# Attention scores as three products of rounded parts, transpositions one step later, and the first gates rounded earlier

## The chip, the cores and the metric

One core of a Trainium2 chip runs the whole kernel in one launch. TensorE multiplies, VectorE and ScalarE work element by element and empty TensorE's accumulation banks (PSUM, four pairs of 1024 columns), GpSimd (POOL) adds a little, and SyncE (SP) issues most transfers. Each engine works off its own list in order and waits for the others by semaphores. The metric is the device time of the kernel in microseconds, the median of several runs. Matrix operands are 32-bit floats in two kinds of product: plain fp32, and fp32r, a faster form with a shorter significand.

## The reference, cut to what matters

The kernel computes two layers of a hybrid trunk for 512 latent tokens and 128 context tokens of width 1024. In each layer a modulated norm feeds one wide projection; four mixers run on its parts (attention A, a gated recurrence B, differential attention C, a gated recurrence D); their outputs are projected, gated and merged, and a convolutional feed-forward part follows. The change is in the two attentions:

```python
s = jnp.einsum('bqgrd,bkgd->bgrqk', qblk.astype(jnp.float32), kf) * scale
p = jax.nn.softmax(s, axis=-1)
return jnp.einsum('bgrqk,bkgv->bqgrv', p, vf)
```

A latent query sees 512 latent keys and 256 cached ones (768), a context query the 128 context keys. A has four heads of 64 channels; C has four heads, each with two softmaxes of 32 channels whose difference weighs the values.

## The kernel before

**Products of parts.** The large matrix products take each fp32 operand as a rounded value (hi) plus its rest (lo), both fp32r, and add hi x hi, hi x lo and lo x hi. ScalarE writes a weight's hi, VectorE the rest. Products with few columns, the attention scores among them, are plain fp32. Only a weight that has been loaded, rounded and subtracted can be used: `early_unit(n)` (ScalarE) and `early_lo(n)` (VectorE) do that for the first six gate weights, one unit of 1024 columns each.

**The attention loop.** The attentions of one layer are 30 steps g = 6 i + u: five blocks i of 128 queries, and six jobs u, the first two for pairs of heads of A, the other four for heads of C. Each step has two score matrices, one per accumulation pair 0 and 1, and their operands lie on different partitions (64 rows each for A, 32 for C). Steps 0 to 23 have 768 keys, steps 24 to 29 have 128. A step's work goes:

- `scores(g)` on TensorE, when the exponentials of step g - 1 have read both score pairs (L1004: 512 latent keys, L1006: 256 cached keys, L1001: context);
- `maxima(g)` on VectorE, the negated maximum of each row (L2143);
- `exponentials(g)` on ScalarE, with the row sums (L1569);
- `normalise(g)` on VectorE (L2150 to L2156); a step of C combines its two matrices to one, a step of A keeps two;
- `turn(g, first)` and, for u = 0 and 1, `turn(g, second)` on TensorE: transposition by blocks of 128 into pair 2 (L1019), each of which waits until ScalarE has copied the one before (`keep_turned`, L1581);
- `weigh(g)` on TensorE, except for u = 2 and 4, whose turn is weighed with the next one: the values are weighed into the lower half of pair 3 (L1035); `outputs` copies them out (VectorE, L2161).

**What fills TensorE between them.** The first six of the gate products, 16 parts each (eight per half of the 640 tokens, a part being three fp32r products of 320 columns, L971 to L973), are done in between. All halves go to the upper half of pair 3 (`HALF_GATE`), so each waits for ScalarE's copy of the half before (L1560, `gates_kept`). `FIRST_FILL` parts go ahead of the loop, and `GATE_FILL` says how many at two places in each step. What is left follows the loop. Behind the stage comes the merge (L791 to L793).

**Order on the engines**, written out by hand. TensorE in step g:

```python
scores(g); turn(g - 2, 1); weigh(g - 3); gate_fill(g, 0); turn(g - 1, 0); gate_fill(g, 1)
```

ScalarE: copies of finished halves (with the next unit's rounding), `keep_turned(g - 2, 1)`, `exponentials(g)`, `keep_turned(g - 1, 0)`. VectorE: the rest of a unit if due, `outputs` if due, `normalise(g - 1)`, `maxima(g)`. Ahead of the loop, in and behind the last projection chunk, run `decay(d)` and `decay_in(d)`, which make the decay factors of mixer D through a chain of ScalarE and VectorE operations that ends at L1546; the loops of ScalarE and VectorE begin behind it. `ada_turn` and `modulation_late` finish a conditioning row; the first gate part waits for the latter (L1977).

Of the kernel before, what the change touches and what calls it, by code (L numbers as in the profile page):

```python
# [8 lines left out]
ALU = mybir.AluOpType  # L9
# [3 lines left out]
P = 128  # L13
D = 1024
KT = D // P
# [188 lines left out]
GATE_FILL, FIRST_FILL = ((0, 2), (1, 2), (1, 2)), 8  # L204
# [45 lines left out]
def halves_before(g):  # L250

    return min(2 * N_EARLY, (FIRST_FILL + sum(sum(GATE_FILL[i % 3]) for i in range(g))) // KT)
# [35 lines left out]
def build(nc, A, O):  # L288
    ctx = ExitStack()
    with ctx:  # L290
# [9 lines left out]
        def sem(name):  # L300
# [123 lines left out]
        W_FIRST = W_EARLY, BIG_R[:, 4608:4864]  # L424
        MIX_AT = NG - 2
# [26 lines left out]
        s_full, nmax_ready, p_ready, normed_p, pt_full, pt_kept, pv_done, o_taken = (  # L452
            sem(n) for n in ("s_full", "nmax_ready", "p_ready", "normed_p", "pt_full", "pt_kept", "pv_done", "o_taken"))
# [25 lines left out]
        HALF_GATE = PS[:, 3, 512:512 + HALF]  # L479

# [281 lines left out]
        def _(pe):  # L762
# [3 lines left out]
            for l in range(DEPTH):  # L766
# [190 lines left out]
                decay(1)  # L957
                if turned is not None:
                    ada_turn(turned)

                def gate_parts():

                    for n in range(N_EARLY):
                        w_hi, w_lo = tiles_of(W_GATE[(EARLY + n) % N_SLOT]), raw(RING_R, EARLY + n, 0, P, P, KT)
                        for h, (a, b, _) in enumerate(HALVES):
                            if h == 0:
                                lo_ready(U_MIX + n)
                            if n + h:
                                pe.wait_ge(half_kept, l * 2 * N_EARLY + 2 * n + h)
                            for k in range(KT):  # L970
                                release(pe.matmul(HALF_GATE, w_hi[:, k, :], h_hi(k)[:, a:b], start=k == 0, stop=False), h + k == 0)  # L971
                                pe.matmul(HALF_GATE, w_hi[:, k, :], h_lo(k)[:, a:b], start=False, stop=False)
                                ins = pe.matmul(HALF_GATE, w_lo[:, k, :], h_hi(k)[:, a:b], start=False, stop=k == KT - 1)  # L973
# [6 lines left out]
                def gate_fill(g, n):  # L980
                    for _ in range(GATE_FILL[g % 3][n]):
                        next(gates, None)
# [9 lines left out]
                def scores(g):  # L992
# [334 lines left out]
        def _(act):  # L1327
# [17 lines left out]
            for l in range(DEPTH):  # L1345
# [134 lines left out]

                def head_inv_root(i):
# [5 lines left out]
                for c in range(NC_Z):  # L1487
                    for n, (g, kind, dst, j) in enumerate(Z_TILES[c]):
# [38 lines left out]
                def early_unit(n):  # L1527
                    chunk_in(EARLY + n)
                    act.activation(W_GATE[(EARLY + n) % N_SLOT], RING[:, (EARLY + n) % N_SLOT, 0:1024], ACT.Copy).then_inc(hi_made, 1)

                early_unit(0)
# [10 lines left out]
                act.dma_start(O["keysT"][at].rearrange("l p a t -> p (l a) t"), ZT[:, AK:AK + 3, TS:T]).then_inc(stored, 16)  # L1542
                act.dma_start(O["vals"][at].rearrange("l p n -> p (l n)"), V_AC[:, NT - 1, :]).then_inc(stored, 16)
# [6 lines left out]
                def gates_kept(count):  # L1550

                    nonlocal halves
                    while halves < count:
                        n, h = divmod(halves, 2)
                        act.wait_ge(half_gate, l * 2 * N_EARLY + halves + 1)
                        if h == 0 and n + 1 < N_EARLY:
                            early_unit(n + 1)
                        if n == 4 and h == 0:
                            act.wait_ge(gate_sent[0], l * 16 + 16)
                        act.activation(LOGIT[n][:, HALVES[h][0]:HALVES[h][1]], HALF_GATE, ACT.Copy).then_inc(half_kept, 1)  # L1560
# [33 lines left out]
                act.wait_ge(al_ready, l * 2 + 2)  # L1594
                for g in range(NG + 3):
# [3 lines left out]
                    keep_turned(g - 2, 1)  # L1599
# [1055 lines left out]
```

## Time and profile before

| what | value |
|---|---|
| median of 3 runs | 2473.71 us (2473.59 to 2474.51) |
| the profiled execution's own time | 2473.59 us |
| its span | 2471.8 us |
| TensorE products busy | 2369.9 us, 96% of the span |
| VectorE, ScalarE, GpSimd busy | 60%, 41%, 12% |
| mean granted clock of TensorE | 0.989 |

The span is the time from the first to the last instruction. In the timeline a row is a start, a duration, an engine, a source line and what was written from what; rows of TensorE overlap, since the duration holds the way through the array, so the difference of two starts tells what a product costs. An fp32 product leaves two records. A bracket is idle time of that engine ahead of the row, and whose work ended it.

### The profile page before, as it was taken

Reading aid. Unit: us, or ns where it says so; the run is one execution under the profiler, and the core shown is the slowest. Engines: PE = TensorE matmul, PEld = TensorE weight load, DVE = VectorE, ACT = ScalarE, POOL = GpSimd, SP = SyncE. Lnnn points to the kernel's source line nnn. Section 1 sums busy time; section 2 is a strip of 40 time slices with the busy share of each in tenths; the row PEclk is TensorE's granted clock in tenths of the full one; section 3 lists DMA queues with packets and bytes.
Section 4 is the critical chain, followed back from the end, with each engine's and each line's share of the span. In section 5 each row is a group of like instructions: output and inputs, shape, how many; then the busy total and the mean of one; then the engine's idle time right before and its main releaser. Section 6 shows DMA issues by size and latency. Waiting matters only on the chain. (4 is left out here: it accounts for less than half of the span.)

```text
span 2471.8 us, 49604 instructions
## 1 busy us (share of the span) xinstructions
PE 2369.9 (96%) x21594; PEld 2209.5 (89%) x21594; DVE 1489.5 (60%) x2274; ACT 1014.9 (41%) x1408; POOL 305.6 (12%) x203
## 2 busy tenths in 40 slices
PE   5999899999999999999989998999999999999998
PEld 4999777889999899999989996788899989999998
DVE  4134476986744788883241436777775658888621
ACT  4245465322252555551143536642212545555410
POOL 0000000000000545530000000000000006555000
PEclk8999999999999999999999999999999999999999
DMA  8555111222246223333244331121222633332321
GB/s 276 186 169 172 51 33 46 59 54 54 60 144 186 79 81 87 86 105 91 75 145 128 119 104 38 33 69 44 55 66 83 207 104 86 86 86 75 103 81 66
DMA packets 326509, 239.32 MB, mean 97 GB/s; under 512 B 18272, under 2 KB 317344, under 8 KB 325024
## 3 DMA queue, kind: packets, MB, share of 16 engines
q1 hardware_dynamic: 317584, 211.32, 29.3%
q10 hardware_dynamic: 8720, 24.99, 2.9%
q8 instruction: 162, 2.65, 0.4%
q14 instruction: 43, 0.35, 0.0%
HBM read 220.68 MB, written 15.60 MB: 96 GB/s over the span
## 5 line engine op out<-in xcount | busy, mean ns | idle before, releaser
L791 PE MATMUL PS<-HH_split,WHI_split 128*128 128x320 f32 x1952 | 616.5, 316 | 12.0 <-DVE HL_split L2017 10.4
L793 PE MATMUL PS<-HH_split,RING_split 128*128 128x320 f32 x1920 | 594.6, 310 | 0.0
L792 PE MATMUL PS<-HL_split,WHI_split 128*128 128x320 f32 x1760 | 545.9, 310 | 0.0
L791 PEld LDWEIGHTS PS<-HH_split,WHI_split 128*128 128x128 f32 x1952 | 368.3, 189 | 24.3 <-issue 13.2
L2042 DVE TENSOR_TENSOR RING_split<-RING,WHI_split 128x1024 fp32r<-128x1024 f32 (+2 forms) x154 | 222.7, 1448 | 270.1 <-ACT WHI_split L1710 183.2
L793 PEld LDWEIGHTS PS<-HH_split,RING_split 128*128 128x128 f32 x1920 | 361.8, 188 | 0.0
L792 PEld LDWEIGHTS PS<-HL_split,WHI_split 128*128 128x128 f32 x1760 | 332.6, 189 | 0.3
L792 PE MATMUL PS<-ZT_split,WHI_split 128*128 128x320 f32 x1032 | 320.5, 311 | 0.0
L741 POOL TENSOR_TENSOR BIG<-HH_split,HL_split 128x640 f32<-128x640 f32 x8 | 14.3, 1824 | 1760.1 <-DVE HL_split L2014 1760.1
L2049 DVE TENSOR_TENSOR RING_split<-RING,WHI_split 128x1024 fp32r<-128x1024 f32 x52 | 62.2, 1223 | 226.3 <-ACT WHI_split L1408 225.9
L792 PEld LDWEIGHTS PS<-ZT_split,WHI_split 128*128 128x128 f32 x1032 | 195.4, 189 | 0.0
L1242 PE MATMUL PS<-BIG_split,WHI_split 128*128 128x320 f32 x576 | 178.0, 309 | 0.0
L791 PE MATMUL PS<-V_split,WHI_split 128*128 128x320 f32 x480 | 151.8, 316 | 1.8 <-DVE RING_split L2042 1.8
L793 PE MATMUL PS<-V_split,RING_split 128*128 128x320 f32 x488 | 152.0, 312 | 0.0
L1710 ACT ACTIVATE WHI_split<-RING 128x1408 fp32r<-128x1408 f32 x32 | 44.1, 1379 | 220.9 <-PE PS L793 168.6
L1241 PE MATMUL PS<-V_split,WHI_split 128*128 128x320 f32 x432 | 133.7, 309 | 0.0
L1646 ACT ACTIVATE WHI<-PS 128x640 f32<-128x640 f32 x48 | 33.8, 705 | 223.9 <-PE PS L793 223.5
L1569 ACT ACTIVATE BIG<-PS,NMX 128x768 f32<-128x768 f32 (+1 forms) x120 | 94.1, 791 | 74.0 <-DVE NMX L2143 73.9
L1242 PEld LDWEIGHTS PS<-BIG_split,WHI_split 128*128 128x128 f32 x576 | 108.1, 188 | 0.0
L2246 DVE COPY_PREDICATED BIG<-MASK,PS 128x640 f32<-128x640 uint8 x96 | 84.5, 881 | 34.9 <-PE PS L1121 34.7
L2143 DVE TENSOR_REDUCE NMX<-PS 128x1 f32<-128x768 f32 (+1 forms) x120 | 93.2, 818 | 15.9 <-PE PS L1006 12.8
L1609 ACT ACTIVATE WHI_split<-RING 128x1280 fp32r<-128x1280 f32 (+1 forms) x54 | 67.0, 1241 | 68.1 <-PE PS L793 68.1
(321 smaller groups left out, 5493.8 us busy)
## 6 DMA issues: line engine op xcount, KB each, us to landing
RING<-in_w_in SPq DMA_DIRECT2D x96, 512.0 KB, 4.0
RING<-in_w_up SPq DMA_DIRECT2D x88, 512.0 KB, 5.0
RING<-in_w_ada SPq DMA_DIRECT2D x80, 512.0 KB, 6.1
RING<-in_w_down SPq DMA_DIRECT2D x32, 384.0 KB, 3.6
RING<-in_w_in SPq DMA_DIRECT2D x40, 256.0 KB, 3.3
RING<-in_w_down SPq DMA_DIRECT2D x32, 320.0 KB, 4.0
RING<-in_w_out SPq DMA_DIRECT2D x16, 512.0 KB, 4.8
ZT<-in_w_ada SPq DMA_DIRECT2D x8, 1024.0 KB, 9.3
```

The lines of the kernel that those rows point to most:

```text
L791: release(pe.matmul(out, w_hi, hi[:, a:b], start=begin, stop=False), fresh and a == 0)
L792: pe.matmul(out, w_hi, lo[:, a:b], start=False, stop=False)
L793: ins = pe.matmul(out, w_lo, hi[:, a:b], start=False, stop=end)
L1241: release(pe.matmul(out, w_hi[k], hi[:, k, :], start=not onto and k == 0, stop=False, skip_group_check=onto), fresh and k == 0)
L1242: pe.matmul(out, w_hi[k], lo[:, k, :], start=False, stop=False, skip_group_check=onto)
L1569: act.activation(PROB[g % 3][m][:, 0:n], pair(m)[:, 0:n], ACT.Exp, bias=NMX[:, g % 3, m:m + 1], accum_out=SUMS[:, g % 3, m:m + 1]).then_in ...
L1609: act.activation(W2[m % 2][:, 0:width], RING[:, (MIX + m) % N_SLOT, 0:width], ACT.Copy).then_inc(hi_made, 1)
L1710: act.activation(W_DN[q % 2], RING[:, (DOWN + q) % N_SLOT, 0:11 * P], ACT.Copy).then_inc(hi_made, 1)
L2042: nv.tensor_tensor(rest, value, as_f32(hi), ALU.subtract).then_inc(lo_made, 1)
L2049: nv.tensor_tensor(z_raw(RING_R, l, c, j), z_raw(RING, l, c, j), as_f32(w_z(u, 256 if kind in ("t4", "t1") else P)), ALU.subtract).then_in ...
L2143: nv.tensor_reduce(NMX[:, g % 3, m:m + 1], pair(m)[:, 0:keys(g // NS) * P], AX.X, ALU.max, negate=True).then_inc(nmax_ready, 1)
L2246: ins = nv.copy_predicated(SCORE[:, h], m, ps)
```

## The change

The scores of the steps with 768 keys become three products of parts: keys and queries are rounded to hi, their rests written in place. The keys (three tiles, a latent and a cached piece each) and the first three queries are rounded in the last projection chunk, the others in the loop; the space of the keys' hi comes from weight buffers and from a state array, whose one block is cleared again in `states`. The first two gate weights are rounded in that chunk too. The second half of the first gate goes to the upper half of pair 2, and its eight parts go behind the first scores. In each step the transpositions come one step later, and the weighing behind them; VectorE takes the maxima ahead of the normalisation. Two stores that ScalarE issues move into the loop.

```diff
-GATE_FILL, FIRST_FILL = ((0, 2), (1, 2), (1, 2)), 8
+FIRST_FILL = 8
+GATE_FILL = ((8, 0),) + ((0, 2), (1, 2), (1, 2)) * 8 + ((0, 2),) * 8
...
+        K_TILE = (AK, CK, CK + 1)
+        K_HI = [(WHI_R[:, 3072:3584], WHI_R[:, 3584:3840]), (BIG_R[:, 4608:5120], WHI_R[:, 3840:4096]),
+                tuple(ST_R[:].rearrange("p (d x n) -> p d x n", d=2, x=3)[:, 0, x, 64:320] for x in (slice(0, 2), 2))]
+        K_LO = [(ZT_R[:, t, 0:TS], CACHE_R[:, PAST * n:PAST * n + PAST]) for n, t in enumerate(K_TILE)]
+        Q_HI = [ST_R[:, 960 + 320 * b:960 + 320 * b + P] for b in range(3)]
...
+        SECOND_HALF = PS[:, 2, 512:512 + HALF]
+        def half_out(n, h):
+            return SECOND_HALF if (n, h) == (0, 1) else HALF_GATE
...
 @@ TensorE, behind the projection
-                decay(1)
                 if turned is not None:
                     ada_turn(turned)
+                decay(1)
 @@ TensorE, gate_parts
-                            if n + h:
+                            if n:
                                 pe.wait_ge(half_kept, l * 2 * N_EARLY + 2 * n + h)
 @@ TensorE, scores
-                    for m in range(2):
-                        pe.matmul(pair(m)[:, 0:TS], ZT[r[m], q, ti], ZT[r[m], k, 0:TS], start=True, stop=True)
-                    for m in range(2):
-                        pe.matmul(pair(m)[:, TS:TS + PAST], ZT[r[m], q, ti], KTC[r[m], kc, :], start=True, stop=True).then_inc(s_full, 1)
+                    n = q_at(i, u)
+                    if g == 0:
+                        pe.wait_ge(k_lo, l * 6 + 6)
+                    pe.wait_ge(q_lo, l * N_Q + (n + 1))
+                    q_hi_part, q_lo_part = Q_HI[n % 3], ZT_R[:, q, ti]
+                    for part, out in ((0, slice(0, TS)), (1, slice(TS, TS + PAST))):
+                        hi_part, lo_part = K_HI[kc][part], K_LO[kc][part]
+                        for first, (qp, kp) in zip((True, False, None), ((q_hi_part, hi_part), (q_hi_part, lo_part), (q_lo_part, hi_part))):
+                            for m in range(2):
+                                ins = pe.matmul(pair(m)[:, out], qp[r[m]], kp[r[m]], start=first is True, stop=first is None)
+                                if first is None and part == 1:
+                                    ins.then_inc(s_full, 1)
 @@ TensorE, turn
                     if t:
                         pe.wait_ge(pt_kept, l * NTURN + t)
+                    else:
+                        pe.wait_ge(half_kept, l * 2 * N_EARLY + 2)
 @@ TensorE, loop over the steps
-                    turn(g - 2, 1)
+                    turn(g - 3, 1)
+                    gate_fill(g, 0)
+                    turn(g - 2, 0)
                     weigh(g - 3)
-                    gate_fill(g, 0)
-                    turn(g - 1, 0)
                     gate_fill(g, 1)
 @@ ScalarE, last projection chunk, behind its first tile
                             decay_in(0)
+                            early_unit(0)
+                            keys_hi()
+                            for k in range(3):
+                                query_hi(k)
+                            early_unit(1)
 @@ ScalarE, loop over the steps
-                    keep_turned(g - 2, 1)
+                    keep_turned(g - 3, 1)
                     if g < NG:
                         exponentials(g)
-                    keep_turned(g - 1, 0)
+                    keep_turned(g - 2, 0)
+                    if q_made(g) is not None:
+                        query_hi(q_made(g))
+                    if g == 3:
+                        act.dma_start(O["keysT"][at].rearrange("l p a t -> p (l a) t"), ZT[:, AK:AK + 3, TS:T]).then_inc(stored, 16)
+                    if g == 4:
+                        act.dma_start(O["vals"][at].rearrange("l p n -> p (l n)"), V_AC[:, NT - 1, :]).then_inc(stored, 16)
+                    if early < N_EARLY and 2 * early - 1 <= halves_before(g):
+                        early_unit(early)
+                        early += 1
  @@ VectorE, loop over the steps
-                    while early < N_EARLY and 2 * early - 1 <= halves_before(g - 1):
+                    if g > NS and g % NS == 3:
+                        outputs(g // NS - 1, 1)
+                    if g < NG:
+                        maxima(g)
+                    if g:
+                        normalise(g - 1)
+                    if g % NS == 5:
+                        outputs(g // NS, 0)
+                    if g and q_made(g - 1) is not None:
+                        query_lo(q_made(g - 1))
+                    if early < N_EARLY and 2 * early - 1 <= halves_before(g - 1):
                         early_lo(early)
                         early += 1
-                    if g % NS == 5:
-                        outputs(g // NS, 0)
-                    if g > NS and g % NS == 3:
-                        outputs(g // NS - 1, 1)
-                    if g:
-                        normalise(g - 1)
-                    if g < NG:
-                        maxima(g)
 @@ VectorE, states
+                    if x + d == 0:
+                        step.mark(nv.memset(ST[:, 0, :, NT - 1, :], 0.0))
```

In `gate_parts` the products write `half_out(n, h)` in place of `HALF_GATE`. `early_unit(0)` stood behind the last projection chunk, `early_unit(n + 1)` in `gates_kept`, the two stores ahead of ScalarE's loop. VectorE runs `early_lo(0)`, `keys_lo()`, three `query_lo` and `early_lo(1)` where ScalarE runs their counterparts; `early_lo(0)` stood behind the chunk too. The new `keys_hi` and `query_hi` are copies on ScalarE (six pieces, 512 and 256 columns; a query 128), `keys_lo` and `query_lo` the subtractions on VectorE. `q_made(g)` names the query that step g rounds, at u = 0, 1, 3 and 5.

## Rows read from the trace of the kernel before

**Rows 1.** The page's first line: span and instructions.

```profile
span 2471.8 us, 49604 instructions
```

**Rows 2.** Timeline, TensorE, steps 19 and 20: start, us, engine, line, operation, count, idle time.

```profile
380.83 1.13 PE L1004 MATMUL PS<-ZT 64*128 64x512 f32 x4
...
385.35 1.13 PE L1004 MATMUL PS<-ZT 32*128 32x512 f32 x4 [0.78 <-ACT BIG L1569]
386.31 0.60 PE L1006 MATMUL PS<-CACHE,ZT 32*128 32x256 f32 x4
386.84 0.87 PE L1019 MATMUL PS<-CONST,BIG 128*128 128x128 f32 x6
387.64 1.09 PE L1035 MATMUL PS<-WHI,V 128*64 128x128 f32 x16
...
389.10 0.41 PE L971 MATMUL PS<-HH_split,RING_split 128*128 128x320 f32 x1
...
389.65 0.82 PE L1019 MATMUL PS<-CONST,BIG 128*128 128x128 f32 x6
390.22 0.39 PE L971 MATMUL PS<-HH_split,RING_split 128*128 128x320 f32 x1
...
391.28 0.70 PE L1004 MATMUL PS<-ZT 32*128 32x512 f32 x2
```

**Rows 3.** Timeline, TensorE: first scores of steps 0, 1, 2, 6, 24; the merge's first product.

```profile
282.42 1.13 PE L1004 MATMUL PS<-ZT 64*128 64x512 f32 x4
...
289.53 2.08 PE L1004 MATMUL PS<-ZT 64*128 64x512 f32 x4 [2.64 <-ACT BIG L1569]
...
295.51 1.13 PE L1004 MATMUL PS<-ZT 32*128 32x512 f32 x4
...
315.61 0.70 PE L1004 MATMUL PS<-ZT 64*128 64x512 f32 x2 [0.78 <-ACT BIG L1569]
...
406.34 0.49 PE L1001 MATMUL PS<-ZT 64*128 64x128 f32 x4 [0.79 <-ACT BIG L1569]
...
428.83 0.42 PE L791 MATMUL PS<-HH_split,WHI_split 128*128 128x320 f32 x1 [0.53 <-ACT WORK L1560]
```

**Rows 4.** Stretch table: us, busy time of each engine, granted clock, DMA share, GB/s.

```profile
280.00:290.00 10.00, 5.58 (x33) 4.25 (x34) 4.97 (x7) 7.25 (x12) 0.00 (x0) 0.88 0.32 93
```

**Rows 5.** Timeline, VectorE, step 19: the two maxima.

```profile
382.43 1.82 DVE L2143 TENSOR_REDUCE NMX<-PS 128x1 f32<-128x768 f32 x2 [0.26 <-PE PS L1006]
```

**Rows 6.** Timeline, TensorE, input projection: products three apart, of 320 and 256 columns.

```profile
149.72 0.31 PE L791 MATMUL PS<-HH_split,WHI_split 128*128 128x320 f32 x1
...
150.16 0.31 PE L791 MATMUL PS<-HH_split,WHI_split 128*128 128x320 f32 x1
...
154.88 0.28 PE L914 MATMUL PS<-RING_split,HH_split 128*128 128x256 f32 x1
...
155.24 0.28 PE L914 MATMUL PS<-RING_split,HH_split 128*128 128x256 f32 x1
```

**Rows 7.** Timeline, TensorE: one fp32 product of 512 columns alone.

```profile
275.21 1.12 PE L780 MATMUL PS<-ZT,WAL 32*128 32x512 f32 x2
```

**Rows 8.** Timeline, weight loads of TensorE, scores of step 19.

```profile
380.83 0.30 PEld L1004 LDWEIGHTS PS<-ZT 64*128 64x128 f32 x4 [0.30 <-ACT BIG L1569]
381.37 0.19 PEld L1006 LDWEIGHTS PS<-CACHE,ZT 64*128 64x128 f32 x2 [0.24 <-issue]
```

**Rows 9.** Timeline, TensorE, step 2: two transpositions without a weighing between them.

```profile
297.00 0.88 PE L1019 MATMUL PS<-CONST,BIG 128*128 128x128 f32 x6
297.63 0.39 PE L971 MATMUL PS<-HH_split,RING_split 128*128 128x320 f32 x1
...
298.87 0.84 PE L1019 MATMUL PS<-CONST,BIG 128*128 128x128 f32 x6 [0.55 <-ACT WHI L1581]
```

**Rows 10.** Timeline, ScalarE and VectorE: the last projection tile.

```profile
275.32 0.70 ACT L1500 ACTIVATE ZT<-PS 128x640 f32<-128x640 f32 x1 [4.97 <-PE PS L793]
...
276.05 0.82 DVE L2112 TENSOR_TENSOR ZT<-ZT,PS 128x640 f32<-128x640 f32 x1 [6.22 <-ACT ZT L1500]
```

More of the change, by code:

```diff
@@ L202 @@
 NG = NT * NS
-GATE_FILL, FIRST_FILL = ((0, 2), (1, 2), (1, 2)), 8
+FIRST_FILL = 8
+GATE_FILL = ((8, 0),) + ((0, 2), (1, 2), (1, 2)) * 8 + ((0, 2),) * 8
+assert FIRST_FILL + sum(map(sum, GATE_FILL)) == 16 * N_EARLY
 TURN0 = [8 * (g // NS) + (0, 2, 4, 5, 6, 7)[g % NS] for g in range(NG)] + [8 * NT]
@@ L250, in halves_before @@
 def halves_before(g):
-    return min(2 * N_EARLY, (FIRST_FILL + sum(sum(GATE_FILL[i % 3]) for i in range(g))) // KT)
+    return min(2 * N_EARLY, (FIRST_FILL + sum(sum(GATE_FILL[i]) for i in range(g))) // KT)
 def keys(i):
@@ L424, in build, with q_at, q_made @@
         W_FIRST = W_EARLY, BIG_R[:, 4608:4864]
+        K_TILE = (AK, CK, CK + 1)
+        K_HI = [(WHI_R[:, 3072:3584], WHI_R[:, 3584:3840]), (BIG_R[:, 4608:5120], WHI_R[:, 3840:4096]),
+                tuple(ST_R[:].rearrange("p (d x n) -> p d x n", d=2, x=3)[:, 0, x, 64:320] for x in (slice(0, 2), 2))]
+        K_LO = [(ZT_R[:, t, 0:TS], CACHE_R[:, PAST * n:PAST * n + PAST]) for n, t in enumerate(K_TILE)]
+        K_RAW = [(ZT[:, t, 0:TS], KTC[:, n, :]) for n, t in enumerate(K_TILE)]
+        Q_TILES = (AQ, AQ + 1, CQ, CQ + 1)
+        Q_HI = [ST_R[:, 960 + 320 * b:960 + 320 * b + P] for b in range(3)]
+        N_Q = 4 * (NT - 1)
+        def q_at(i, u):
+            return 4 * i + (0, 1, 2, 2, 3, 3)[u]
+        def q_made(g):
+            i, u = divmod(g, NS)
+            k = {0: 4 * i + 3, 1: 4 * i + 4, 3: 4 * i + 5, 5: 4 * i + 6}.get(u)
+            return k if k is not None and k < N_Q else None
         MIX_AT = NG - 2
@@ L980, in gate_fill @@
                 def gate_fill(g, n):
-                    for _ in range(GATE_FILL[g % 3][n]):
+                    for _ in range(GATE_FILL[g][n]):
                         next(gates, None)
@@ L1479, in decay_in, with early_unit, keys_hi, query_hi @@
                     act.activation(SQ[d], pair(2)[:, 0:T], ACT.Abs, bias=COLS[:, C_AB + d:C_AB + d + 1]).then_inc(al_lin, 1)
+                def early_unit(n):
+                    chunk_in(EARLY + n)
+                    act.activation(W_GATE[(EARLY + n) % N_SLOT], RING[:, (EARLY + n) % N_SLOT, 0:1024], ACT.Copy).then_inc(hi_made, 1)
+                def keys_hi():
+                    act.wait_ge(params_in, (l + 1) * N_PARAM)
+                    for n in range(3):
+                        for part in range(2):
+                            out, raw_part = K_HI[n][part], K_RAW[n][part]
+                            if n == 2 and part == 0:
+                                raw_part = raw_part.rearrange("p (x n) -> p x n", n=PAST)
+                            act.activation(out, raw_part, ACT.Copy).then_inc(k_hi, 1)
+                def query_hi(k):
+                    i, t = divmod(k, 4)
+                    act.activation(Q_HI[k % 3], ZT[:, Q_TILES[t], i * P:(i + 1) * P], ACT.Copy).then_inc(q_hi, 1)
                 def head_inv_root(i):
@@ L2101, in head_rotary, with early_lo, keys_lo, query_lo @@
                     nv.tensor_tensor(ZT[:, t, 0:TS], TMP[0][:, 0:TS], TMP[1][:, 0:TS], ALU.add).then_inc(qk_done, 1)
+                def early_lo(n):
+                    lo(U_MIX + n, RING_R[:, (EARLY + n) % N_SLOT, 0:1024], RING[:, (EARLY + n) % N_SLOT, 0:1024], W_GATE[(EARLY + n) % N_SLOT])
+                def keys_lo():
+                    for n in range(3):
+                        for part in range(2):
+                            rest, value, hi_part = K_LO[n][part], K_RAW[n][part], K_HI[n][part]
+                            if n == 2 and part == 0:
+                                rest, value = (x.rearrange("p (x n) -> p x n", n=PAST) for x in (rest, value))
+                            v.wait_ge(k_hi, l * 6 + (2 * n + part + 1))
+                            nv.tensor_tensor(rest, value, as_f32(hi_part), ALU.subtract).then_inc(k_lo, 1)
+                def query_lo(k):
+                    i, t = divmod(k, 4)
+                    at = slice(i * P, (i + 1) * P)
+                    v.wait_ge(q_hi, l * N_Q + (k + 1))
+                    nv.tensor_tensor(ZT_R[:, Q_TILES[t], at], ZT[:, Q_TILES[t], at], as_f32(Q_HI[k % 3]), ALU.subtract).then_inc(q_lo, 1)
                 sig = 0
@@ L2119, in _ @@
                             head_round_rest(c - QK_AT - 2)
+                        if c == NC_Z - 1 and n == 0:
+                            early_lo(0)
+                            keys_lo()
+                            for k in range(3):
+                                query_lo(k)
+                            early_lo(1)
                     if l + c == 0:
```

27 lines of the change are left out of this document (9 added, 18 removed).

## The prediction, written before the result was known

> **What bounds the kernel now.** I read the page first, then the chain of waits, then the timeline of the attention stage, the only stage that the change alters. The span is 2471.8 us [rows 1], and the profiled execution took 2473.59 us, 1.79 us more; the median of the runs is 2473.71, so the sum below, made against 2473.59, is good for the median to 0.1 us. TensorE is busy nearly everywhere, so time saved in one stage goes straight to the end, if TensorE doesn't wait there instead. In the first layer the stage runs from 282.42 us to the first product of the merge at 428.83; the second layer repeats it, step by step, and I count it twice.
>
> Two limits alternate from step to step. In step 19 TensorE has little to do and waits 0.78 us for the exponentials [rows 2]: scores, two maxima of 1.82 us [rows 5], two exponentials, and only then the next scores, because both score buffers are in use. That loop is 385.35 - 380.83 = 4.52 us, of which 1.49 are the scores (385.35 to 386.84 in step 20), so everything else in it is 3.03. In step 20 TensorE is full: scores 1.49, transposition 0.80, weighing 1.46, one gate part 0.55, transposition 0.57, two parts 1.06, together 5.93, and no wait [rows 2]. Steps 6 to 23 take 406.34 - 315.61 = 90.73 us, 30.24 for six [rows 3]. The start of the stage is worse: steps 0 to 5 take 33.19, because step 0 takes 7.11 and step 1 5.98 [rows 3]. Before step 1 TensorE waits 2.64 us; the granted clock in this stretch is 0.88 [rows 4], and the first scores of step 1 take 2.08 us where those of step 2 take 1.13, nearly the ratio of the 1.2 and 2.4 GHz levels. The reader is to see a stage with four wait-free steps in six [rows 2, 3], and a start with a stall and a slow stretch after it.
>
> **The scores by parts.** One step's scores are now four fp32 products in two pairs, the two of a pair on different rows of the array. A pair of 512 columns takes 385.35 to 386.31, 0.96 us, and the pair of 256 to 386.84, 0.53 [rows 2]. A single fp32 product of 512 columns takes as long as such a pair: 1.12 us in its row [rows 7] against 1.13. So the two of a pair run side by side. Of the 0.96, 0.11 is the first weight load (four loads of 0.19 begin within 0.11 [rows 8]) and 0.85 the stream, 2048 column cycles at 2.4 GHz; of the 0.53, 0.43 is stream and 0.10 the change to the next shape.
>
> The change makes six pairs of these two, in fp32r. Three fp32r products take 0.44 us at 320 columns and 0.36 at 256 [rows 6], 0.147 and 0.120 each, so about 0.42 ns a column more: 0.228 at 512. No fp32r product on part of the rows is in this trace. From below: 0.11 + 3 x 0.213 + 3 x 0.107 + 0.10 = 1.17 us, streams without any gap. From above, if pairs stay side by side with the gaps of the full array: 0.11 + 3 x 0.228 + 3 x 0.120 + 0.10 = 1.25. If 0.11 and 0.10 were both hidden, 1.04. If pairs don't run side by side at all, 0.11 + 6 x 0.213 + 6 x 0.107 + 0.10 = 2.13. I take 1.20, since the rows of the fp32 pairs show neither a gap nor a lost overlap. That is 0.29 less than 1.49.
>
> The loads for the 256-column products begin at 381.37, in the middle of the 512-column streams on the same rows, which end at about 381.8 [rows 2, 8]; so I count only the first load. The Trainium skill has a rule that speaks against this ("TensorE: Matmul & The Clock Gate", Part 3: Packing small matmuls, row/col tiling): a weight load overlaps products in flight only when it goes to another row group. By that rule every pair's loads would be exposed, and the sum would be rival C's; the trace disagrees.
>
> **Transpositions one step later.** What was transposition (second), weighing, parts, transposition (first) becomes transposition (second of g-3), 0 or 1 part, transposition (first of g-2), weighing, two parts. The buffer of the transposed block is single, so the second of two transpositions waits until ScalarE has copied the first. In the old order the weighing of 1.46 us covers the copy. Where it didn't, in step 2, the next transposition starts 1.87 us after the first although only 0.63 + 0.55 lies between them [rows 9]. In the new order nothing but that part covers it in the steps u=3 and u=4 of each six (those with two transpositions). A transposition right ahead of a weighing costs 0.17 more than ahead of a part (0.80 against 0.63 [rows 2, 9]), so 0.74 behind a part or a wait (0.57 + 0.17).
>
> The six steps are then, S being 1.20: u=0 and u=2: S + 0.55 + 0.74 + 1.46 + 1.06 = 5.01 each, TensorE-bound. u=1 and u=5: TensorE has S + 1.69 and S + 2.18, less than the loop, so S + 3.03 = 4.23 each. u=3 and u=4: S + 1.87 + 0.74 + 1.46 + 1.06 = 6.33 each. Together 31.14 against 30.24: 0.90 more for six, though the scores give 6 x 0.29 = 1.74 back; the new wait (0.69 and 1.24 us), and the loop that was reached in two steps already, take it. Three such sixes cost 2.7 us a layer. Maxima ahead of the normalisation take VectorE's normalisation out of the loop; it was beside the scores already, so I count nothing: a gain up to 0.4 us a step if it isn't, and a loss of none.
>
> **The start.** Step 0 gets eight gate parts of 0.44 us (0.147 x 3 [rows 6]) that wait for no copy, since they write another bank. It becomes 1.20 + 3.52 + about 0.1 = 4.8 in place of 7.11; two units of weight are rounded beforehand, so the maxima of step 0 no longer stand behind one. Step 1 becomes the loop, 4.23 in place of 5.98; with TensorE busy through step 0 the clock has no reason in these rows to fall. Step 2 is a loop step too, 4.23; steps 3 to 5 are 6.33 + 6.33 + 4.23. Sum 30.2 against 33.19: 3.0 less a layer.
>
> **Rounding keys and queries.** ScalarE rounds two weight units of 1024 columns (one was rounded here before, just behind the tile), six pieces of keys and three queries; VectorE makes as many subtractions. All lie in the last projection chunk, where ScalarE idles 4.97 us and VectorE 6.22 [rows 10]. At the 640-column rows there, 0.70 and 0.82 us, nine pieces of at most 512 columns are under 6.3 and 7.4 us, by columns (2688) about 3.0 and 3.4; with the units (2048 columns, 2.2 and 2.6) 5.2 and 6.0. They about fit, and the unit no longer rounded behind the tile pays for an overrun. I take 0; from -0.6 to +1.0 a layer. The queries' rounding in the loop (128 columns, 13 a layer on each engine) falls on waits; 0, at worst 13 x 0.2. The two stores that ScalarE issues move from ahead of the stage to steps 3 and 4, behind its work there: 0, at worst 1.3. ada_turn ahead of decay(1): 0. TensorE gets three new waits with its whole order queued behind each: for the rounded keys (done with the chunk), for a query's rest (made two steps or more before its use) and, ahead of the first transposition, for the second half's copy (ScalarE's first work in step 1): none comes last. The fill in states, 192 columns, about 0.25 us a layer on VectorE: 0 to 0.25.
>
> **The end.** Steps 24 on, 406.34 to 428.83 = 22.5 us [rows 3], lose five gate parts (2.2 us) and gain the same kind of waits, short ones. I take -0.7, between -2.2 and +0.5.
>
> **Sum.** -3.0 + 2.7 - 0.7 = -1.0 us a layer, -2.0 for both: 2473.59 - 2.0 = 2471.6 us. All 24 steps carry S once, so each 0.1 us of S is 2.4 us a layer, 4.8 in all. The result is no change that can be told: 0.2%, 4.9 us, is about what a measurement of this kernel tells from none.
>
> **Rivals.**
> *A. Scores at their floor.* With S = 1.05 (load and shape change hidden) the sum is 2471.6 - 7.2 = 2464.4. For it: the loads of a pair begin together [rows 8]. Against: the fp32 pairs don't hide them.
> *B. Weight loads in a row (slower).* In each of the six pairs the loads follow one another, 12 x 0.12 + 0.10 = 1.54: +0.34 x 48 = 16, so 2488. It decides from S = 1.34 upward. For it: fp32r has one load for half the streaming that fp32 had. Against: [rows 8].
> *C. Every load exposed.* If no load went beside a stream on its own rows, the six pairs would each wait 0.11: S = 6 x 0.11 + 0.96 + 0.10 = 1.72, +25, so 2497. Against: [rows 2, 8]. It is what the rule of the skill named above would give.
> *D. Pairs not side by side.* S = 2.13: +45, so 2516. Against: [rows 7].
> *E. The clock falls within the sixes.* TensorE now idles about 1.3, 0.9, 0.7 and 1.2 us in each 31 us. One fall cost 5.98 - 4.52 = 1.5; three a layer make +9, so 2480. Against: no wait there is near 2.64 [rows 3].
> *F. The start isn't gained.* If the rounding ahead delays the decay's exponentials, step 0 stays at 7.11 less 0.29: +2.0 a layer, 2476. This is also the case that the change doesn't do what it says.
>
> **Chances.** The sum 0.40 (its own range 2467 to 2477), A 0.27, B 0.09, C 0.03, D 0.05, E 0.07, F 0.09. Faster by over 0.2%: A and 0.06 of the sum, 0.33. Within: 0.30 of the sum, 0.06 of F and 0.01 of E, 0.37. Slower: 0.04 of the sum, B, C, D, 0.06 of E and 0.03 of F, 0.30. The range runs from 2461, A with a start that gives 1.7 us a layer more, to 2487, just under B; it leaves out C, D and most of B.
>
> **What would show it.** Scores of a step: start to the next operation 1.20 (1.05 A, 1.54 B, 1.72 C, 2.13 D). In steps u=3 and u=4 an idle time of TensorE ahead of the second transposition, put down to ScalarE's copy, 0.7 and 1.2 us. Steps u=1 and u=5 at 4.23. Step 1 starting 4.8 us after step 0 and a granted clock near 1 there. Six steps at 31.1. The prediction is wrong if S is outside 1.13 to 1.34, or if the second transposition doesn't wait.

## The result, and the profile after

The changed kernel takes 2479.76 us (median of 20 executions) against 2474.56 of the kernel before: ratio 1.0026, 95% interval 1.0019 to 1.0032. It is slower by 5.2 us, where no change was forecast; the time lies inside the forecast's range, on rival E's value (2480).

The profiled execution of the changed kernel took 2483.09 us, 3.3 above its median; its span is 9.5 us longer than the one before (to be read beside [rows 1]):

```profile
span 2481.3 us, 50122 instructions
```

The starts of steps 0, 6 and 24 and of the merge in the first layer (timeline of TensorE, beside [rows 3]):

```profile
285.11 0.50 PE L1038 MATMUL PS<-WHI_split,ST_split 64*128 64x512 f32 x2
...
316.40 0.50 PE L1038 MATMUL PS<-WHI_split,ST_split 64*128 64x512 f32 x2 [0.78 <-ACT BIG L1620]
...
412.59 0.38 PE L1027 MATMUL PS<-ZT 64*128 64x128 f32 x2 [0.78 <-ACT BIG L1620]
...
434.71 0.41 PE L817 MATMUL PS<-HH_split,WHI_split 128*128 128x320 f32 x1 [0.53 <-ACT WORK L1611]
```

From the first scores to the merge are 149.6 us, before 146.4; in the second layer 149.3 and 146.4. Ahead of that, the eight gate parts of the first layer ran at half clock in this execution: they start at 278.70, as before, and the scores behind them at 285.11 in place of 282.42. Within the start a second stretch at half clock stands in step 2, behind an idle time of 1.88 us (at full clock a transposition takes 0.8 to 0.9):

```profile
294.33 0.49 PE L1038 MATMUL PS<-BIG_split,ST_split 32*128 32x512 f32 x2 [1.88 <-ACT BIG L1620]
...
297.00 1.48 PE L1055 MATMUL PS<-CONST,BIG 128*128 128x128 f32 x6
```

Steps 19 (its scores and the transposition behind them) and 20, beside [rows 2]:

```profile
384.53 0.50 PE L1038 MATMUL PS<-WHI_split,ST_split 64*128 64x512 f32 x2
...
385.57 0.28 PE L1038 MATMUL PS<-WHI_split,ZT_split 64*128 64x256 f32 x2
385.77 0.33 PE L1055 MATMUL PS<-CONST,BIG 128*128 128x128 f32 x1
...
388.80 0.50 PE L1038 MATMUL PS<-BIG_split,ST_split 32*128 32x512 f32 x2 [1.26 <-ACT BIG L1620]
...
390.61 1.48 PE L1055 MATMUL PS<-CONST,BIG 128*128 128x128 f32 x6
392.02 1.98 PE L1071 MATMUL PS<-WHI,V 128*64 128x128 f32 x16
```

The scores take 385.77 - 384.53 = 1.24 us, close to the 1.20 forecast. But step 20 has a transposition of 1.48 us where others have 0.8 to 0.9, and a weighing of 1.98 where [rows 2] has 1.09. The table by stretches shows why, a granted clock near half (us, then busy time of TensorE, its weight loads, VectorE, ScalarE and GpSimd, then granted clock, DMA share, GB/s; the first stretch is the eight parts, the second this place):

```profile
278.70:285.00 6.30, 6.30 (x24) 6.22 (x24) 1.56 (x2) 4.69 (x7) 0.00 (x0) 0.52 0.33 83
390.00:394.00 4.00, 4.00 (x31) 3.60 (x31) 3.04 (x5) 2.58 (x5) 0.00 (x0) 0.57 0.43 146
```

The new wait stands in steps 21 and 22 (u=3 and u=4) as forecast, the second transposition behind ScalarE's copy of the first:

```profile
396.73 0.87 PE L1055 MATMUL PS<-CONST,BIG 128*128 128x128 f32 x6
...
398.60 0.84 PE L1055 MATMUL PS<-CONST,BIG 128*128 128x128 f32 x6 [0.55 <-ACT WHI L1632]
...
403.16 0.88 PE L1055 MATMUL PS<-CONST,BIG 128*128 128x128 f32 x6
405.02 0.84 PE L1055 MATMUL PS<-CONST,BIG 128*128 128x128 f32 x6 [0.99 <-ACT WHI L1632]
```

In what follows a "six" is the six steps u=0 to u=5, three of them a layer in steps 6 to 23; it is "slow" when one of its steps runs partly at half clock, and "clean" otherwise. Step lengths in us, from the starts of the scores in the timelines:

| kernel | u=0 | 1 | 2 | 3 | 4 | 5 | six |
|---|---|---|---|---|---|---|---|
| before | 4.74 | 4.51 | 5.93 | 5.43 | 5.12 | 4.51 | 30.24 |
| forecast | 5.01 | 4.23 | 5.01 | 6.33 | 6.33 | 4.23 | 31.14 |
| changed | 5.08 | 4.27 | 5.07 | 6.43 | 6.42 | 4.26 | 31.53 |
| changed, slow | 5.08 | 4.27 | 6.67 | 6.43 | 6.42 | 4.26 | 33.13 |

### The profile page after: what moved, and what is told of

It reads as the page before. It is cut to its first block and busy times, and to the rows that moved or that the text cites. A ratio compares the mean times of both kernels' runs of the same rounds, so it can differ in the third digit from the quotient of the medians.

```text
span 2481.3 us, 50122 instructions
## 1 busy us (share of the span) xinstructions
PE 2370.8 (96%) x21786; PEld 2231.7 (90%) x21786; DVE 1496.2 (60%) x2320; ACT 1026.2 (41%) x1452; POOL 305.7 (12%) x203
```

## The experiments

The first group takes the changed kernel and fills or orders TensorE's work otherwise. Ratios are to the kernel before, measured alongside.

**Parts between the transpositions.**

```
-GATE_FILL = ((8, 0),) + ((0, 2), (1, 2), (1, 2)) * 8 + ((0, 2),) * 8
+GATE_FILL = ((8, 0),) + ((0, 2), (1, 2), (3, 0), (2, 0), (1, 2), (1, 2)) * 4 + ((0, 2),) * 8
```

> The changed kernel with one table altered: in the steps u=3 and u=4 all gate parts of the step (three and two) stand between the two transpositions, none behind the weighing. Nothing is added or taken away. Theory: the second transposition waits for ScalarE's copy of the first (0.55 to 1.24 us in the trace of the changed kernel, six steps take 31.5 us), and that idle time of TensorE is also what ends in a fall of the clock (one weighing of 1.98 in place of 1.09 us in each layer, 1.6 us). Then u=3 goes from 6.43 to about 5.8, u=4 from 6.43 to about 5.4, six steps to 29.9, and four sixes in two layers give 13, without the clock falls 16: 2464 to 2467 us. Rival 1, the exponentials' loop is what sets these steps and the idle time only moves ahead of the next scores: six steps stay above 31, 2477 to 2480. Rival 2, the waits go but the clock falls have another reason: 2467, with a slow weighing still in each layer.

Measured: 2468.36 us, ratio to before 0.9971 (0.9962 to 0.9980), 1.4 us over the theory's 2464 to 2467. Steps u=3 and u=4 take 5.50 and 5.35, a clean six 29.54. The second transposition waits no more (no idle time on its row, which starts 0.45 us behind the last part):

```profile
361.15 0.31 PE L997 MATMUL PS<-HH_split,RING_split 128*128 128x320 f32 x1
...
361.60 0.82 PE L1055 MATMUL PS<-CONST,BIG 128*128 128x128 f32 x6
```

So the wait lengthened these steps, and 2.0 us a six of it was avoidable by the layout alone. The clock part of the theory fails and rival 2 holds: four of six sixes still have a u=2 of 6.6 to 6.7.

**Parts moved to the steps that wait for the loop.** The table's middle part becomes `((0, 4), (0, 2), (2, 0), (2, 0), (0, 4), (0, 2)) * 4` for u=1, 2, 3, 4, 5, 0.

> As the kernel with all parts between the transpositions, and besides parts are taken from the steps in which TensorE is full and given to u=1 and u=5, where it waits for the exponentials: four each in u=1 and u=5, two in every other step (in u=3 and u=4 between the transpositions). Theory: the full steps are bound by TensorE, so u=0 and u=2 go from 5.08 to 4.5, u=3 and u=4 from 6.43 to 5.3, u=1 and u=5 stay at 4.27 to 4.4; six steps 28.3 in place of 31.5, some 3.2 x 3 + 2.1 = 11.7 a layer, with the clock falls 13: 2453 to 2457 us. Rival, the loop over ScalarE and VectorE sets the steps once TensorE has less: six steps not under 29.9, 2464 or more.

Measured: 2457.41 us, 0.9926 (0.9912 to 0.9939), at the upper end of the forecast; a six takes 28.87, half a microsecond over it (u=0 stays at 5.04), and no six is slow. The idle time ahead of u=2 is 0.37 us.

**Idle time filled in u=3 and u=4.** In these steps one and two gate parts are computed again behind `gate_fill(g, 0)`.

> The changed kernel with idle time of TensorE filled and nothing else altered: between the two transpositions of u=3 and u=4 one and two gate parts are computed once more (three products each; in u=3 the repeated part is added to its sum twice, so five of sixteen early gate sums are not the reference's). The lengths of the steps should stay, since the repeats lie in the wait for ScalarE's copy (0.55 and 1.24 us against 0.44 and 0.99): six steps 31.4 to 31.7. Theory, the idle time is what brings the clock down in the middle of the sixes: no weighing at half clock in steps 6 to 23, 1.6 us a layer less, 2476 to 2477. Rival, these falls come without regard to the idle time: still one or more slow weighings in a layer and 2479 to 2481. Second rival, the repeats cost their own time: 2.5 to 4 us a layer more, 2485 or more.

Measured: 2482.27 us, 1.0033 (1.0022 to 1.0043); a clean six takes 31.53, so the repeats add nothing to it, and still two of six have a slow u=2. The theory falls: with the waits between the transpositions filled, the clock falls as before.

**Decay ahead of the turned row.**

```
+                decay(1)
                 if turned is not None:
                     ada_turn(turned)
-                decay(1)
```

> The changed kernel with one edit undone: the decay's two products stand ahead of the turning of the modulation row again, as before. Theory: in the first layer the new order leaves TensorE with nothing but fp32 products of few columns or few rows ahead of the wait for the modulation, and the first eight gate parts then run at half clock (0.267 us a product against 0.147); with the order undone they run at full clock, the first scores start 2.3 us earlier, 2477.5 us. Rival: the order has no part in it (the idle time of 1.4 to 1.6 us ahead of the parts is nearly the same in both kernels, and the clock falls or not by what lies further back), the time stays at 2479 to 2481 and the parts run at half clock in some executions of either order.

Measured: 2481.42 us, 1.0027 (1.0017 to 1.0037). The rival holds: no gain. The first of the eight parts of the first layer takes 0.63 us in the first profile of the changed kernel and at most 0.42 in all sixteen others, its own second one (below) among them: half-clock parts came once, and no run shows why.

**Idle time filled in u=1.** At the end of each u=1 in steps 0 to 23 the last part is computed twice more.

> The changed kernel with one idle time of TensorE filled and nothing else altered: at the end of the steps u=1 the step's last gate part is computed twice more (two times 0.44 us into an idle time of 1.26; the part is added to its sum three times, so eight of the early gate sums are not the reference's). Theory: in every trace so far the slow weighing of the sixes stands in step u=2, some 2 us behind this idle time, and in the kernel that gives u=1 two more parts no six has one; so it is this idle time, the longest of the six, that is followed by the fall. Then steps u=2 take 5.07 everywhere, and with step lengths unchanged the time is 3 to 5 us under the changed kernel: 2475 to 2477. Rival: the fall goes to another place (u=3, u=0) and the time stays at 2479 to 2482.

Measured: 2474.07 us, 0.9998 (0.9989 to 1.0007), 0.9 us under the theory's range. No six is slow; each takes 31.5. Step 20, to be read beside its rows above:

```profile
385.53 0.50 PE L1057 MATMUL PS<-BIG_split,ST_split 32*128 32x512 f32 x2 [0.39 <-ACT BIG L1639]
...
387.31 0.82 PE L1074 MATMUL PS<-CONST,BIG 128*128 128x128 f32 x6
388.06 1.09 PE L1090 MATMUL PS<-WHI,V 128*64 128x128 f32 x16
```

TensorE does more work and the kernel is faster. The repeats stand in step 1 too, where they shorten the idle time ahead of step 2 from 1.88 to 1.00 us, and that step is not slow here either. The granted clock of steps 6 to 23 of the first layer, this kernel's row:

```profile
313.14:407.70 94.56, 86.48 (x811) 72.37 (x811) 68.50 (x110) 57.71 (x116) 0.00 (x0) 1.00 0.11 31
```

and the changed kernel's, 1.6 us longer with fewer products:

```profile
316.40:412.59 96.19, 85.45 (x793) 71.16 (x793) 68.57 (x110) 57.71 (x116) 0.00 (x0) 0.98 0.12 31
```

**One repeat only.** As above with `range(1)`.

> The changed kernel with the last gate part of each step u=1 computed once more, not twice (eight early gate sums are not the reference's): the idle time ahead of u=2 is about 0.82 us, as long as that ahead of u=0 (0.78), behind which no profile shows a fall. Theory: no slow step u=2, 2473 to 2476, as with two repeats. Rival: the chance falls with the idle time but not to nothing, one or two of six, 2476 to 2478.

Measured: 2473.95 us, 0.9997 (0.9987 to 1.0007), no slow six. No fall follows the idle time of 0.82 us:

```profile
354.05 0.50 PE L1057 MATMUL PS<-BIG_split,ST_split 32*128 32x512 f32 x2 [0.82 <-ACT BIG L1639]
355.84 0.82 PE L1074 MATMUL PS<-CONST,BIG 128*128 128x128 f32 x6
356.59 1.09 PE L1090 MATMUL PS<-WHI,V 128*64 128x128 f32 x16
```

The second group takes the change apart.

**Transpositions and maxima as before.** TensorE's order is again `turn(g - 2, 1)`, weighing, parts, `turn(g - 1, 0)`, with ScalarE's copies to match, and VectorE normalises ahead of the maxima. The scores by parts and the new gate table stay.

> The changed kernel with the order of transpositions and of maxima and normalisation put back as before (the second transposition and the first each one step earlier, the weighing between them, normalisation ahead of the maxima); the scores by three products, the early rounding and the second half's bank stay. Theory: the scores by parts gain 0.25 us in every step, and what took it away is the later turn alone. Then each step is as before less 0.25: six steps 28.7 (before 30.24, changed 31.5), steps 0 to 5 about 28.7, so 9 us a layer less than before: 2455 us (2451 to 2460). Rival: the old order can't use shorter scores, since its steps are bound by ScalarE and VectorE: six steps 29.9 or more, 2465 to 2472.

Measured: 2460.20 us, 0.9942 (0.9928 to 0.9955), just over the theory's range of 2451 to 2460. A clean six is 29.52, not 28.7, and four of six are slow, again in u=2 alone, behind the same idle time:

```profile
350.89 0.50 PE L1038 MATMUL PS<-BIG_split,ST_split 32*128 32x512 f32 x2 [1.26 <-ACT BIG L1620]
...
352.18 1.54 PE L1055 MATMUL PS<-CONST,BIG 128*128 128x128 f32 x6
353.65 1.94 PE L1071 MATMUL PS<-WHI,V 128*64 128x128 f32 x16
```

**Start alone.** As the one above, and the scores are the four fp32 products a step of the kernel before, with no rounding of keys and queries.

> Only the start of the change is left: plain fp32 scores, the old order of transpositions and maxima, and of the change the two units rounded ahead, the eight parts in step 0, the second half's bank and the later stores. Theory: steps 0 to 5 go from 33.2 to about 30.3 us, sixes as before (30.24), 3 us a layer: 2468 us (2465 to 2470). Rival: the fall of the clock that came behind the wait of step 0 comes elsewhere in the start, and only half is gained: 2471 to 2474.

Measured: 2469.13 us, 0.9969 (0.9957 to 0.9982). Steps 0 to 5 take 30.0 and 30.1, as forecast; but a six is 30.75, half a microsecond over the kernel before. The new gate table, which this kernel keeps, puts its pattern one step later, three parts in u=0 and two in u=1; u=0 is 0.4 us longer, and the idle time at the end of u=1, ahead of the scores of u=2, grows from 0.78 to 1.26. No six is slow.

**Plain scores, later transpositions.** The changed kernel with the four fp32 products a step of the kernel before, without the rounding of keys and queries; all else stays.

> The changed kernel with plain fp32 scores and without the rounding of keys and queries; the later transpositions, maxima first and the start stay. Theory 1, on length: each of the 24 steps carries 0.25 us more, six steps 33.0 in place of 31.5, 6 us a layer, so 12 more than the kernel in which no clock fall is left (2474): 2486 us. Theory 2, on the clock: the fall in step u=2 needs both the idle time of 1.26 us ahead of it and the scores by parts; the kernel with plain scores and the old order has that idle time (1.26) and no slow step in six sixes, the one with scores by parts and the old order has it (1.27) and four. Then no step u=2 here shows a slow weighing though the idle time is there. Rival: the idle time alone does it, and two to four sixes show 1.6 us more in u=2: 2489 to 2492.

Measured: 2494.19 us, 1.0071 (1.0058 to 1.0084). A clean six is 33.0, as theory 1 says; theory 2 falls, four of six have a slow u=2 with plain scores. The time is 2 us over the rival's range as well.

**VectorE's order alone.** The changed kernel with normalisation ahead of the maxima again.

> The changed kernel with VectorE's order put back alone: normalisation of the step before ahead of the maxima. Theory: the normalisation (1.3 us) lies beside the scores (1.24) and the loop hardly changes, steps u=1 and u=5 at 4.27 to 4.6, the time within 4 us of the changed kernel: 2478 to 2484. Rival: maxima first is what holds the loop at 4.27, and without it every loop step takes 0.3 to 0.5 more and the waits of u=3 and u=4 grow: 2486 to 2492.

Measured: 2480.18 us, 1.0021 (1.0011 to 1.0030); u=1 and u=5 stay at 4.26, a clean six 31.49. Maxima first is worth nothing beside the later transpositions; the theory holds.

**Old order, new scores, parts laid out by step.** `((0, 5), (0, 1), (0, 2), (0, 2), (0, 4), (0, 2)) * 4` for u=1, 2, 3, 4, 5, 0, on top of the kernel with transpositions and maxima as before.

> The kernel with the old order of transpositions and maxima and the new scores, and the gate parts laid out by step: 5, 1, 2, 2, 4, 2 for u=1, 2, 3, 4, 5, 0, all behind the first transposition. Theory: TensorE is the bound in u=2, 3 and 4 of that order and idle in u=1 and 5, so six steps come to 27.4 to 27.9 and the time to 2447 to 2451 us, the fastest of all. Rival: the loop over exponentials and maxima holds every step at 4.5 or more with the normalisation in it, and nothing is gained over the same order without the new layout: 2453 to 2457.

Measured: 2449.00 us, 0.9889 (0.9874 to 0.9904), the fastest of all, 1.1% under the kernel before. Six steps, 312.10 to 340.19:

```profile
312.10:340.19 28.09, 27.07 (x265) 23.03 (x265) 23.30 (x39) 19.26 (x40) 0.00 (x0) 1.00 0.11 32
```

TensorE is busy for 27.1 of 28.1 us at full clock. A six is a little over the forecast (27.4 to 27.9), the time within it, and no six is slow. Part of the gain over the same order without this layout (0.9942) is the four slow sixes there, 1.6 us each.

The third group takes profiles again and puts the idle time into the kernel before.

**The changed kernel again.**

> The changed kernel itself once more, for a second profile. Theory: the falls of the clock in the sixes stand in steps u=2 again (one to four of the six), other steps repeat to 0.05 us, and the eight parts ahead of the first scores run at half clock or not by chance: 2478 to 2482. Rival: another place, or the half-clock parts of the first layer again, which would make that a fault of the order in this kernel.

Measured: 2481.40 us, 1.0020 (1.0011 to 1.0029). Three of six sixes are slow, all in u=2, other sixes than in the first profile; the parts ahead of the first scores run at clock 1.00. Step 2 of the first layer is slow again, and here the whole step and the parts behind it: the start takes 32.75 us there.

**The kernel before again.**

> The kernel before once more, for a second profile. Theory: its idle time of 0.78 us ahead of u=2 is followed by no fall of the clock: six steps 30.24 six times, the start at 33.2 with its slow stretch behind the wait of step 0: 2472 to 2476. Rival: falls in the sixes here too, which the first profile didn't happen to show; then they are no cost of the change.

Measured: 2475.78 us, 0.9999 (0.9990 to 1.0008). Six sixes of 30.25, the start 33.1 and 33.2: no fall in the sixes, so they came with the change.

**A longer idle time in the kernel before.**

```
-GATE_FILL, FIRST_FILL = ((0, 2), (1, 2), (1, 2)), 8
+GATE_FILL, FIRST_FILL = ((0, 2), (1, 1), (1, 3), (0, 2), (1, 2), (1, 2)), 8
```

(and the index taken modulo 6)

> The kernel before with one table altered: one gate part of each step u=1 goes to the step u=2 that follows, so TensorE's idle time ahead of the scores of u=2 is 1.3 us in place of 0.78; nothing of the change is in it. By length alone u=2 is 0.5 us longer in four sixes of two layers: 4 us, 2479. Theory, an idle time of about 1.26 us there is by itself followed by a fall of the clock in nearly half of the cases (24 of the 54 sixes of nine profiles so far): two to four of six sixes show 1.5 us more in u=2, 2481 to 2485. Rival, the old order with plain scores is spared (none of six in the kernel with the start alone): no six shows it, 2477 to 2480.

Measured: 2477.55 us, 1.0008 (0.9998 to 1.0018). Five sixes of 30.69 and one of 32.27, in the second layer, again in u=2, with nothing of the change in the kernel:

```profile
1534.02 1.13 PE L1004 MATMUL PS<-ZT 32*128 32x512 f32 x4 [1.22 <-ACT BIG L1569]
1535.51 1.02 PE L1019 MATMUL PS<-CONST,BIG 128*128 128x128 f32 x6
1536.47 1.98 PE L1035 MATMUL PS<-WHI,V 128*64 128x128 f32 x16
```

The idle time is enough to make a fall possible, but it came less often than the theory said, and the time stays in the rival's range.

**The start alone again.**

> The kernel with the start alone once more, for a second profile: it has the idle time of 1.26 us ahead of u=2 and its first profile shows no fall in six sixes. Theory, that was chance: two to four of six show a slow step u=2 now. Rival, it is spared: again none; then the idle time is needed but does not suffice.

Measured: 2467.82 us, 0.9978 (0.9964 to 0.9992); none of six slow. The rival holds, none of twelve in all, though the idle time is there and the weighing behind it runs at full clock (first profile):

```profile
354.31 1.13 PE L1032 MATMUL PS<-ZT 32*128 32x512 f32 x4 [1.27 <-ACT BIG L1611]
355.80 0.87 PE L1049 MATMUL PS<-CONST,BIG 128*128 128x128 f32 x6
356.61 1.09 PE L1065 MATMUL PS<-WHI,V 128*64 128x128 f32 x16
```

Counted over all profiles, steps 6 to 23 of both layers: with an idle time of 1.22 to 1.28 us ahead of u=2, 25 of 66 sixes are slow (eleven profiles); with 0.83 us or less there, 0 of 36 (six profiles). Every slow step of the sixes is a u=2.

## Why the prediction was wrong

**The step that failed: the clock.** The prediction saw that TensorE would idle about 1.3 us in each six and gave falls of the clock there 0.07, because the one fall in the trace stood behind 2.64 us. Rival E had the mechanism and the price of a fall (1.5 us; measured 1.6). In the two profiles of the changed kernel 5 of 12 sixes are slow, 4.0 us an execution, and in each the start has one slow step 2 behind 1.88 us of idle time (0.7 and 2.1 us); over all profiles a step 2 behind 1.85 to 1.89 us is slow in 3 of 14 cases. Filling the idle time of u=1 took the ratio from 1.0026 and 1.0020 to 0.9998 and 0.9997, 5 to 7 us: the whole loss, and without the falls the kernel takes the time of the one before. That the time meets rival E's 2480 is in part luck: E counts six falls an execution on top of a sum with 2.0 us of gain; measured were 2.5 in the sixes and one in the start, on top of a stage without that gain. The prediction's own signs of being wrong, S and the wait of the second transposition, both came out right; the clock was not among them.

**Where the idle time comes from.** The 1.3 us of u=1 stands in the prediction's terms, the loop (S + 3.03) less TensorE's own work (S + 1.69), but not why it is longer than the 0.78 us of before. The shorter scores don't explain it, since S is in both terms, and the kernels with plain scores show 1.26 too. The start alone shows the source, not named in the prediction: the gate table, moved by one step, takes a part from u=1 (0.78 to 1.26 us of idle time, and 0.5 us a six by itself).

**The scores.** Right: 1.24 us, forecast 1.20, within the bounds, so A to D are refused. (B's 0.12 us a load stands in no row, but at 1.54 it is refused by a distance.) Between the kernels with the old order a six falls from 30.75 to 29.52, with the later order from 33.0 to 31.5: 1.2 and 1.5 us, 0.21 to 0.25 a step. Loads go in beside products on the same rows, as in step 19, where the first product pair starts at 384.53 and the next at 384.87:

```profile
384.64 0.19 PEld L1038 LDWEIGHTS PS<-ZT_split,ST_split 64*128 64x128 f32 x2
384.87 0.19 PEld L1038 LDWEIGHTS PS<-WHI_split,ZT_split 64*128 64x128 f32 x2
```

The rule of the Trainium skill ("TensorE: Matmul & The Clock Gate", Part 3: Packing small matmuls, row/col tiling), by which, as the prediction reads it, each load would stand alone, would have made it 1.72; the trace decides against it.

**The later transpositions.** The mechanism is right and so is its size: by the starts above the second transposition follows the first after 1.87 and 1.86 us, where 1.87 was forecast. (The brackets, 0.55 and 0.99, are smaller than the forecast waits of 0.69 and 1.24, because they begin at the end of the row before; in [rows 9] too the bracket is 0.55 where the starts give 0.69.) The whole step is 6.43 for 6.33. Taken apart, one clean six is 30.24 + 0.51 (table) - 1.23 (scores) + 2.01 (later transpositions, VectorE's order with them) = 31.53. With the scores by parts the old order gives 2460.20 us and the later one 2479.76: about 20 us in the stage for nothing, of which the clean lengths show 12 in the sixes, 4 in the starts and 2 at the ends. The wait is new: in the old order the weighing stands between the two transpositions, and the second has no idle time ahead of it [rows 2].

**The sum without the clock.** Predicted, for a layer: start -3.0, sixes +2.7, end -0.7, together -1.0. Measured in the kernel with two repeats, which has no fall: start 30.6 and 31.0 against 33.2, so -2.6 and -2.2; sixes 3 x 1.28 = +3.8; end 22.1 against 22.5, -0.4; together +0.8 and +1.2. The sixes are the term most off, 0.4 us each: the scores account for 0.04 x 6 of it, the rest is 0.05 or 0.06 in each of the steps with two transpositions and 0.02 or 0.03 in u=0 and u=2. In the second layer step 0 takes 5.37 us, not 4.8, since the first maxima wait for the decay's last exponential, a small part of what rival F feared:

```profile
1496.50 1.82 DVE L2226 TENSOR_REDUCE NMX<-PS 128x1 f32<-128x768 f32 x2 [0.81 <-ACT ZT L1599]
```

So over two layers the stage is 4 us worse than forecast. About 1 us comes back ahead of it, where the prediction counted nothing: from the last projection product to the first scores the same kernel takes 7.06 and 7.10 us, the one before 7.45 and 7.82. Its ratio (0.9989 to 1.0007) is too wide to tell what is left from the forecast.

**The edits costed at nothing.** Maxima first and the turned row ahead of the decay change nothing that can be told, as forecast (2480.18 and 2481.42 without them). The first scores wait for no rounding: they stand right behind the parts in every profile. But in the first layer the first gate part waits 1.42 us for the conditioning row, and 0.46 in the kernels that round no keys and queries (the start alone, and plain scores): about 1 us there, the upper bound of the prediction's range for the rounding. The two stores were not tested by themselves; their 1.3 us at worst stands in no row.

**What stays open.** Why some kernels are nearly spared. With plain scores and the old order together (the start alone, twice, and the kernel before with a longer idle time) 1 of 18 sixes is slow, in all other kernels with this idle time 24 of 48. Transfers don't decide it: from 1.2 us ahead of the scores of u=2 to 2 us behind their start the DMA share is 0.87 to 0.93 in the start alone, without a fall, and 0.03 at the one fall of the kernel before. No fall in the sixes came without the idle time; what else decides was not found.

## What to carry to other kernels

When a table places filler work, work out the idle time of the bounding engine step by step under the old table and the new one, and look for a long idle time that returns at the same place of every turn; here the table, moved by one step, made 1.26 us of 0.78. Move work into it before anything else. Filler work belongs by table into the steps that wait for another engine, and between two operations that share a buffer; here that layout alone was worth 1.0% with the later order (0.9926 against 1.0026) and 0.5% with the old one (0.9889 against 0.9942), the falls of the clock that it took away included. An edit that reorders a chain around a single buffer should first show which wait it removes: here it removed none and added 2.0 us to a six.

## What the hardware showed that was not expected

An idle time of TensorE of 1.22 to 1.28 us that returns at one place of a loop was followed by a stretch at half clock in 25 of 66 cases, at 1.6 us each, one of 0.83 us or less in none of 36. The length alone does not tell how often: with nearly the same idle time one group of kernels had 1 of 18 and the others 24 of 48, and 1.85 to 1.89 us ahead of step 2 of the start had 3 of 14. The place in the loop is fixed, the turn in which it happens is not: two profiles of the same kernel show it in different sixes. Computing a product again, for no use but to keep TensorE busy, made the kernel 5 to 7 us faster.
